# Joining two weight pieces of each Strassen quarter into one rounding and one subtraction of 2048 columns

## What is computed

```python
def sqrelu_mlp(h, w_in, w_out):
    u = jax.nn.relu(h @ w_in)
    return (u * u) @ w_out

for l in range(DEPTH):                       # DEPTH = 2, D_MODEL = 2048, SEQ = 256, D_FF = 8192
    h = h + (pool_mixer or diff_attention)(rms_norm(h, mix_norm[l]))
    h = h + sqrelu_mlp(rms_norm(h, mlp_norm[l]), w_mlp_in[l], w_mlp_out[l])
    ...
return rms_norm(h, final_norm)
```

## Time and profile before

| | us |
|---|---|
| median of 3 runs (1793.85 to 1796.69) | 1794.84 |
| the profiled execution | 1795.1 |
| its span, first to last instruction | 1793.3 |
| TensorE busy in it | 1782.3 |
| VectorE busy in it | 1476.7 |
| ScalarE busy in it | 1201.4 |

### The profile page before, as it was taken

How to read it: one execution, slowest core, us unless ns; L and a number is a source line. 1 busy time by engine, 2 the same in 40 slices (tenths; PEclk the granted TensorE clock), 3 DMA queues, 4 the chain that set the end, 5 groups by cost and what they waited for, 6 DMA issues and landing times.

```text
span 1793.3 us, 23765 instructions
## 1 busy us (share of the span) xinstructions
PE 1782.3 (99%) x8118; PEld 1478.1 (82%) x8118; DVE 1476.7 (82%) x1495; ACT 1201.4 (67%) x1491; POOL 13.0 (1%) x17
## 2 busy tenths in 40 slices
PE   9999999999999999999999999999999999999998
PEld 7888888788888888888888888888888888888887
DVE  7888999899898987755556777889998989898986
ACT  7677777777777775644435545677777777777773
POOL 0000000000000000000000000000000000000000
PEclk9999999999999999999999999999999999999999
DMA  8555657465556555565554446464655565655562
GB/s 310 181 179 177 238 176 242 150 227 187 202 187 230 190 205 197 184 190 188 191 190 151 142 151 225 144 212 164 232 188 198 186 232 188 228 188 188 193 245 102
DMA packets 178656, 348.65 MB, mean 194 GB/s; under 512 B 10624, under 2 KB 10752, under 8 KB 178176
## 3 DMA queue, kind: packets, MB, share of 16 engines
q1 hardware_dynamic: 177984, 346.02, 56.3%
q10 hardware_dynamic: 576, 1.44, 0.2%
HBM read 345.32 MB, written 2.10 MB: 194 GB/s over the span
## 4 chain that ended last, share of the span: by engine, by line
PE 97%; issue 1%; DVE 1%; DMA 0%; ACT 0%; POOL 0%; SPq 0%; DVEq 0%; POOLq 0%; ACTq 0%
PE bank L1514 12%; PE bank L1515 12%; PE bank L1516 12%; PE bank L1520 12%; PE bank L1521 12%; PE bank L1522 12%; PE bank L1479 7%; PE bank L1481 6%; PE bank L1480 6%; PE bank L1549 1%; PE bank L1506 1%; DMA h<-in_x 0%; PE bank L1828 0%; PE bank L1755 0%; DVE w_lo L960 0%
## 5 line engine op out<-in xcount | busy, mean ns | idle before, releaser
L966 DVE TENSOR_TENSOR w_lo<-raw,w_hi 128x1024 fp32r<-128x1024 f32 x392 | 468.9, 1218 | 3.2 <-ACT w_hi L559 0.3
L565 ACT ACTIVATE w_hi<-raw 128x1024 fp32r<-128x1024 f32 x224 | 236.9, 1058 | 216.6 <-DVE raw L982 134.8
L1520 PE MATMUL bank<-w_hi,u_hi_a 128*128 128x512 f32 x896 | 348.9, 389 | 0.0
L1522 PE MATMUL bank<-w_hi,u_lo_a 128*128 128x512 f32 x896 | 348.7, 389 | 0.0
L1521 PE MATMUL bank<-w_lo,u_hi_a 128*128 128x512 f32 x896 | 348.6, 389 | 0.0
L1514 PE MATMUL bank<-w_hi,mix_hi 128*128 128x512 f32 x828 | 324.7, 392 | 2.2 <-ACT h L683 2.0
L1515 PE MATMUL bank<-w_lo,mix_hi 128*128 128x512 f32 x828 | 322.9, 390 | 0.0
L1516 PE MATMUL bank<-w_hi,mix_lo 128*128 128x512 f32 x828 | 322.9, 390 | 0.0
L960 DVE TENSOR_TENSOR w_lo<-arena,w_hi 128x2048 fp32r<-128x2048 f32 x114 | 257.3, 2286 | 58.7 <-ACT w_hi L553 58.5
L553 ACT ACTIVATE w_hi<-arena 128x2048 fp32r<-128x2048 f32 x114 | 215.8, 1909 | 26.7 <-PE bank L1516 23.6
L542 ACT ACTIVATE w_hi<-raw 128x1024 fp32r<-128x1024 f32 x128 | 133.7, 1062 | 148.5 <-PE bank L1481 143.7
(11 more groups left out here) (198 smaller groups left out, 2301.8 us busy)
## 6 DMA issues: line engine op xcount, KB each, us to landing
raw<-in_w_mlp_in SPq DMA_DIRECT2D x240, 512.0 KB, 4.8
arena<-in_w_mlp_out SPq DMA_DIRECT2D x240, 512.0 KB, 6.2
raw<-in_w_kv SPq DMA_DIRECT2D x64, 512.0 KB, 4.4
raw<-in_w_q SPq DMA_DIRECT2D x32, 512.0 KB, 4.6
raw<-in_w_o SPq DMA_DIRECT2D x32, 512.0 KB, 4.4
arena<-in_w_mlp_in SPq DMA_DIRECT2D x16, 512.0 KB, 6.3
raw<-in_w_mlp_out SPq DMA_DIRECT2D x16, 512.0 KB, 5.1
raw<-in_pool_w SPq DMA_DIRECT2D x4, 512.0 KB, 10.0
```

Source lines behind the costliest of these rows:

```text
L565: nc.scalar.activation(w_hi[:, slot], raw_half[half][:, i], ACT.Copy).then_inc(hi_ready, 1)
L966: nc.vector.tensor_tensor(w_lo[:, slot], raw_half[half][:, i], w_hi[:, slot].bitcast(F32), ALU.subtract).then_inc(lo_ready, 1)
L1520: nc.tensor.matmul(bank[:], hi, w_hi[:, slot, kk, :], start=False, stop=False, skip_group_check=True)
L1522: return nc.tensor.matmul(bank[:], lo, w_hi[:, slot, kk, :], start=False, stop=False, skip_group_check=True)
```

## The change

Steps 1 and 2 of a unit, pieces c and d, go into neighbouring slots. Where step 1's slot is not 7, `hi_pair` and `lo_pair` now do both with one ScalarE and one VectorE operation of 2048 columns; `hi_pair` waits for both landings and raises `hi_ready` by 2. Where it is slot 7, all stays as it was. With the slots of the units, that leaves out one of 4 units in every other pair, 7 of 56.

```diff
@@ mix_hi_lots (ScalarE) @@
                 for step in steps:
                     spot = (slot + step) % HALVES
-                    if step < 3:
+                    if step == 1 and spot < HALVES - 1:
+                        hi_pair(at + 1, spot, half, 1, landed)
+                    elif step == 2 and spot > 0:
+                        continue
+                    elif step < 3:
                         hi_piece(at + step, spot, half, (0, 2, 3)[step], landed)
                     else:
                         hi_sum(at + step, spot, half, (1, 3, 0, 2)[step - 3], sums + step - 2)
@@ mix_lo_lots (VectorE) @@
                 a, b, c, d = (raw_half[half][:, i] for i in range(4))
                 for step in steps:
+                    spot = (slot + step) % HALVES
+                    if step == 1 and spot < HALVES - 1:
+                        lo_pair(at + 1, spot, half, 1)
+                        continue
+                    if step == 2 and spot > 0:
+                        continue
                     if step == 3:
                         dve.wait_ge(w_summed, sums + 1)
                         dve.wait_ge(lo_ready, at + 3)
```

## The result

The changed kernel takes 1822.09 us (1820.97 to 1822.57, 4 runs), the kernel before 1794.38 (1793.85 to 1796.69, 4 runs, one more than in the table above): a ratio of 1.0154, interval 1.0141 to 1.0166. It is 27.7 us slower. Forecast were 1834 us, range 1813 to 1857. The profiled execution took 1821.0 with a span of 1819.2.

A forecast was written before the change was run, and what follows sets the result against it. TensorE was taken to bound the kernel, with VectorE just in front. 45.4 us of new VectorE lateness, less 1.0, 3.9 and 2.0, left 38.5 on 1795.1: 1834 us, range 1813 to 1857.

The forecast's parts named there:

- What bounds: Whole kernel: TensorE, busy 99%, sets the pace; VectorE runs in front with a shortest lead of 0.2 us between pairs.
- The saving is worth nothing: VectorE's joined subtractions save 0.07 us each, 3.4 us in all, on an engine that waits in this stretch.
- The wait and its place: Units k = 1 to 3: VectorE waits for d's landing and the whole wide rounding; 0 to 2.6 us per unit.
- The rival in which only the first term counts: Loads of later units catch up, so only units k = 1 pay: 19 us, 1814 us; chance 12%.
- The size of the term: VectorE's lateness in the 35 units: k = 1 26.2 us, k = 2 7.5, k = 3 11.7; sum 45.4.
- What is absorbed: Lateness swallowed by existing slack: 3.9 us over 13 boundaries, about 2.0 at the layers' first lead and last slack.
- The stall of before: VectorE's 3.53 us idle without releaser, costing 3.9 us at TensorE in the old kernel, was to stay as VectorE lateness.
- The clock: TensorE's half clock after waits falls into time it would have waited anyway, so nothing was added to the forecast.
- the rival with half clock: Stalls at several places of a pair, clock loss uncovered: 23 us over 12 boundaries on top of 38.5, 1857; chance 12%.
- What was to be seen: Signs in the trace: joined subtractions idle some 45 us, TensorE idle 2 to 4 us per pair boundary, u turns 86 to 87 us.

## Why the prediction was right, and by how much not

*What bounds.* Right. TensorE set the pace and VectorE ran just in front: 35.1 us of work put on VectorE alone cost 23.4.

*The saving is worth nothing.* Right where it was put: units k = 0 joined alone moved the time by no more than can be measured. Against the Trainium skill's fixed cost per instruction (VectorE: DVE Perf Modes, section on the TRN2 errata) this is no contradiction, as the saved time is VectorE's and not the kernel's. The Trainium skill's other rule (Perfetto Trace Analysis, Optimizing Scalar/DVE Operations), that breaking up instructions of an engine that is not saturated may help where they cause bubbles on others, is borne out here: with VectorE 81 to 82% busy, the two narrow operations run at 1794.4 us and the joined one at 1822.1.

*The wait and its place.* Right, and shown by parts: only k = 1 to 3, and more by the long rounding than by the landing. With ScalarE's part alone joined, which holds both, the loss is 36.0 us; with the wait for d and a narrow rounding it is 6.1 and 10.5 us. That terms of k = 2 and 3 count as well is shown too: 11.7 us by themselves. The rival in which only the first term counts falls, although its 1814 is the number of units k = 1 alone.

*The size of the term.* "The same reading for each of the 35 units gives ... 45.4", or 47.9 before the 0.07 us each. That counts from where a narrow subtraction in a row would begin, 1.13 us behind the start of the last. The profile counts idle time from the end of the last, at 1.22 us, so the reading is some 44.8 us in the profile's terms. With only these units joined the trace shows 44.9, in the changed kernel 41.5. For k = 1 alone the reading was 25.9 in the same terms and the measurement 27.0, for k = 2 and 3 18.8 and 19.3. The readings taken one by one are thus nearly right. Why the changed kernel's are 3 us less is open: the time from the issue of a unit's first load to the landing of d lay between about 8 and 10 us in the traces and shows no clear order. Units k = 0 were to give back 1.0 us; with the two waits of 0.83 they cost 0.9.

*What is absorbed.* This is the step that was mis-sized most. Forecast were 3.9 us at ScalarE's copy and some 2 at the layers' ends, 5.9 of 44.4 us of lateness. VectorE's wait for that copy, ahead of c_11, in the traces before and after:

```profile
DVE arena L1057 <- ACT arena L641: 37.7, 14, 3.0
```

```profile
DVE arena L1067 <- ACT arena L645: 32.7, 14, 2.9
```

5.0 us were absorbed there, somewhat more than 3.9. In all the changed kernel absorbed 17.1 us: VectorE's lateness was 43.0 us (the 43.2 of waits, with 0.02 us more for each of the 36 subtractions that waited, 1.22 + 2.29 against 3.49 for three in a row, and 0.07 less for the 13 that did not), and the two profiled executions are 25.9 us apart. 3.5 of the 17.1 are the stall, below. Of the other 8.6, 2.1 are the plain lots' at the layers' ends; the rest is spread over VectorE's other waits, at most 1.8 us in any group of instructions, and was not taken apart.

*The stall of before.* "The stall that is there now stays" failed for the profiled executions: VectorE's 3.53 us with no releaser are not in the trace after. A gap of this kind stands at the same place in some of the other traces and not in all. The kernel with k = 2 and 3 joined has one of 1.66 us, shown here, and one of 1.39 us at 336.88:

```profile
331.44 0.69 DVE L1073 TENSOR_TENSOR arena<-bank,arena 128x512 f32<-128x512 f32 x1 [1.66 <-issue]
```

What ended these gaps is not shown. Counted on VectorE alone, the profiled executions add up without the prediction's terms: its idle time rose by 26.7 us (41.1 before the wide subtractions of raw pieces, less 5.0 at the copy, 3.5 of the stall and 5.9 elsewhere), its busy time fell by 0.8, and the spans are 25.9 apart.

*The clock.* The half clock was expected a few us behind each boundary, and by a rival as 23 us on top. It did not come: at the boundaries the granted clock is 1.00. TensorE lost its time in waits of at most 1.4 us, not in one of 2 to 4 as I had written. So the rival with half clock falls for this kernel; what waits of 2 to 4 us at each boundary would do was not run.

*What was to be seen.* The turns of u were to be 86 to 87 us apart; VectorE's c_11 in the trace after comes every 85.2 to 87.5 us, before every 83.4, but for the 87.3 across the stall. Its joined subtractions wait 41.5 us in units k = 1 to 3 where some 45 were named; in units k = 0 none were, and there are two of 0.83. Its busy sum was to fall by 7 us and fell by 0.8, since that sum leaves out where two instructions overlap, and the overlap of two narrow ones is gone as well (1.13 + 1.22 = 2.35 us against 2.29).

No run beats the kernel before. The one part of the change that is free, k = 0, gives nothing.

## What to carry to other kernels

Before two operations are joined, read when each input is there. A joined operation starts when its last input has landed, and its first reader starts when all of it is done: here that was one rounding of 1.9 us behind the later landing, where half of the work had been done in the wait. Where the inputs arrive one by one and the consumers' queue is in order, join only where both are early; and an engine at 82% can be the one that sets the time, as here, where its lead over the busy one is some tenths of a us at one place of each round. In a forecast, the places where an engine already waits need the same care as the new wait: here they took some 17 us of 43 where 5.9 had been allowed.

## What was not expected of the hardware

A wait of TensorE of 2.0 us was followed by a granted clock of 0.50 (1.2 GHz) and cost 3.9 us in all, whereas more than twenty waits of up to 1.4 us in the changed kernel left it at 1.00. The length of the wait alone does not tell: waits of 2.0, 2.4 and 4.6 us at the same place in the kernels with k = 2 and 3, with k = 1 and with ScalarE's part joined were followed by 0.50 as well, but in the kernel that only waits for d one of 2.3 us was not. There the granted clock was 1.00 in every slice behind the restart:

```profile
346.94 0.49 PE L1516 MATMUL bank<-w_hi,mix_hi 128*128 128x512 f32 x1 [2.28 <-ACT h L685]
```

```profile
348.00:349.00 1.00, 1.00 (x6) 0.83 (x5) 0.73 (x2) 1.00 (x3) 0.00 (x0) 1.00 0.00 0
```

VectorE subtracted 2048 columns in 2.29 us against 2 x 1.22, but by the starts in a row the gain is 0.07 us, not 0.15.
